# Cross-attention of a decoder trunk: additions ahead of the maximum, probabilities scaled on ScalarE, value mix in four column groups, query units in turn

## What is computed

```python
def mem_xattn(h, mk, mv, wq, wo):
    q = (h @ wq).reshape(b, L, XA_HEADS, XA_HEAD_DIM)
    s = einsum('blhd,bmhd->bhlm', q, mk) * XA_HEAD_DIM ** -0.5
    p = softmax(s, axis=-1)
    o = einsum('bhlm,bmhd->blhd', p, mv).reshape(b, L, D_MODEL)
    return o @ wo

x = x + mixer(rmsnorm(x)); x = x + mem_xattn(rmsnorm(x), ...)
```

## Time and profile before

| | us |
|---|---|
| median of 3 runs | 2808.32 |
| the runs | 2815.7, 2808.32, 2801.9 |
| the profiled execution | 2788.76 |
| its span, first to last instruction | 2786.6 |
| mean granted TensorE clock in it | 0.952 of 2.4 GHz |

### The profile page before, as it was taken

One profiled execution on the slowest core, in us unless ns is written; L12 is line 12 of the kernel. 1 busy time (PEld: TensorE's weight loads), 2 busy tenths in 40 slices (PEclk: granted clock), 3 DMA queues, 4 the chain that ended last, 5 costly groups with the idle time before them and its releaser, 6 DMA issues.

```text
span 2786.6 us, 38288 instructions
## 1 busy us (share of the span) xinstructions
PE 2486.7 (89%) x15517; PEld 2338.8 (84%) x15517; DVE 1469.3 (53%) x2201; ACT 586.2 (21%) x1123; POOL 847.7 (30%) x415
## 2 busy tenths in 40 slices
PE   5989999999999887887998899989989986988787
PEld 5989999999999877776887898889779876867775
DVE  4464553332333546546665745656575666545654
ACT  3431110000000321113223303221330233221113
POOL 0034443334433322221223333333323232412220
PEclk7999999999999999998999999999999997999998
DMA  4641111111111132221101121211112011232221
GB/s 143 203 129 50 42 49 46 46 45 45 45 45 50 36 130 90 77 98 51 49 21 54 51 60 31 65 32 46 46 57 55 22 46 49 99 101 80 80 78 74
DMA packets 242704, 182.20 MB, mean 65 GB/s; under 512 B 6125, under 2 KB 229629, under 8 KB 241503
## 3 DMA queue, kind: packets, MB, share of 16 engines
q1 hardware_dynamic: 197592, 124.87, 15.1%
q10 hardware_dynamic: 44975, 55.41, 5.8%
HBM read 159.97 MB, written 20.98 MB: 65 GB/s over the span
## 4 chain that ended last, share of the span: by engine, by line
PE 75%; DVE 15%; ACT 4%; issue 3%; POOL 1%; DMA 1%; ACTq 0%; SPq 0%; DVEq 0%; POOLq 0%
PE acc L792 33%; PE acc L817 12%; PE acc L991 6%; PE acc L1019 4%; PE acc L917 2%; PE M L1146 2%; PE acc L1225 2%; PE acc L1236 2%; DVE cache L2132 2%; PE acc L1088 2%; PE M L1067 1%; PE acc L1241 1%; DVE x L2056 1%; PE acc L841 1%; PE acc L1229 1%
## 5 line engine op out<-in xcount | busy, mean ns | idle before, releaser
L649 POOL TENSOR_TENSOR w_hi<-w_raw,zero 128x1024 fp32r<-128x1024 f32 x153 | 298.2, 1949 | 1645.9 <-PE acc L792 669.0
L792 PE MATMUL acc<-h_hi,w_hi 128*128 128x344 f32 x2232 | 506.1, 336 | 31.7 <-POOL w_lo L652 21.0
L792 PE MATMUL acc<-h_lo,w_hi 128*128 128x344 f32 x2232 | 481.4, 325 | 0.0
L792 PE MATMUL acc<-h_hi,w_lo 128*128 128x344 f32 x2232 | 476.9, 322 | 0.0
L792 PEld LDWEIGHTS acc<-h_hi,w_hi 128*128 128x128 f32 x2232 | 383.7, 192 | 57.3 <-issue 34.0
L652 POOL TENSOR_TENSOR w_lo<-w_raw,w_hi 128x1024 fp32r<-128x1024 f32 x153 | 395.0, 2582 | 12.0
L792 PEld LDWEIGHTS acc<-h_lo,w_hi 128*128 128x128 f32 x2232 | 385.5, 193 | 0.0
L792 PEld LDWEIGHTS acc<-h_hi,w_lo 128*128 128x128 f32 x2232 | 378.2, 191 | 0.0
L1871 DVE TENSOR_TENSOR x<-acc,x 128x1032 f32<-128x1032 f32 x96 | 117.9, 1231 | 242.0 <-PE acc L817 242.0
L991 PE MATMUL acc<-y_hi,w_hi 128*128 128x344 f32 x384 | 129.8, 338 | 61.5 <-DVE x L2056 57.7
L991 PEld LDWEIGHTS acc<-y_hi,w_hi 128*128 128x128 f32 x384 | 73.2, 191 | 73.5 <-DVE x L2056 59.5
(11 more groups left out here) (307 smaller groups left out, 4673.9 us busy)
## 6 DMA issues: line engine op xcount, KB each, us to landing
w_raw<-in_w_in_even SPq DMA_DIRECT2D x48, 512.0 KB, 3.6
w_raw<-in_w_in_odd SPq DMA_DIRECT2D x41, 512.0 KB, 3.7
cache<-in_cache_mem_k ACTq DMA_DIRECT2D x8, 2048.0 KB, 7.4
cache<-in_cache_mem_v ACTq DMA_DIRECT2D x8, 2048.0 KB, 7.7
w_raw<-in_w_xa_k SPq DMA_DIRECT2D x16, 512.0 KB, 4.3
w_raw<-in_w_xa_v SPq DMA_DIRECT2D x16, 512.0 KB, 3.9
w_raw<-in_w_out_even SPq DMA_DIRECT2D x16, 512.0 KB, 3.7
w_raw<-in_w_xa_q SPq DMA_DIRECT2D x16, 512.0 KB, 3.9
```

Of the source, the lines that this page charges most:

```text
L649: pool.tensor_tensor(hi, raw_ap, zcol.to_broadcast([P, width]), ALU.add).then_inc(w_hi_done, 1)
L792: ins = pe.matmul(acc[a][:, n * 512:n * 512 + CH], wt[:, s, w], mv[:, k, n * CH:(n + 1) * CH], start=(k == 0 and j == 0), stop=(k == KT - ...
```

## The change

Seven edits, all of them in cross-attention:

- VectorE runs `outputs_out` of a slot ahead of the slot's maximum, no longer behind it; the last two jobs of a head (piece 8) are added in slot 6, straight behind the second copy of the mix, and not in slot 7.
- The scaling of the probabilities by 1/sum goes from VectorE (L2114) to ScalarE, behind the exponential of the next tile and ahead of the copy of pt_hi.
- SAMPLE is spread otherwise: the middle heads begin the products in slot 4 with one token and end with two each in slots 8 and 9; the last head takes one in each of slots 3 to 6 and two each in 7 and 8. Its load of the cached values is issued one slot later.
- The mix with the cached values goes to four column groups: sample token b = 2j + r is computed in rows 32j to 32j+31 of the bank, four matmuls with weights of 32 columns stand next to each other in the program, each for another group. `spt` becomes 32 columns wide per token and lies in q_bc's place; VectorE zeroes it once per head (128x512) and not once per layer.
- The copy behind the mix takes 128 rows, and the turning matmuls (L1152) pick 8 of them.
- The two query units run one behind the other, with `token_sums` between them.
- The memset of spt at the start of each layer's attention is gone.

```diff
-SAMPLE = {... "middle": (0, 0, 0, 2, 1, 1, 1, 1, 1, 1), "last": (0, 0, 0, 2, 2, 2, 2, 0, 0, 0)}
+SAMPLE = {... "middle": (0, 0, 0, 0, 1, 1, 1, 1, 2, 2), "last": (0, 0, 0, 1, 1, 1, 1, 2, 2, 0)}
...
-                for b in range(NB):
+                for r in range(2):
                     for m in range(MT):
-                        ins = pe.matmul(M0[0:NB, 0:HD], spt[:, m, b * NB:(b + 1) * NB], cache[:, b * MT + m, :],
-                                        start=(b == 0 and m == 0), stop=(b == NB - 1 and m == MT - 1))
+                        for j in range(NB // 2):
+                            b = 2 * j + r
+                            ins = pe.matmul(M0[32 * j:32 * j + 32, 0:HD], spt[:, m, b, :], cache[:, b * MT + m, :],
+                                            start=(r == 0 and m == 0), stop=(r == 1 and m == MT - 1))
...
-                project_pair((0, 1), attended, KT * (n_th - 1), sums)
+                project(0, attended, KT * (n_th - 1))
+                sums()
+                project(1)
...
+                        if 1 <= i <= TT:
+                            j = i - 1
+                            act.wait_ge(rinv_ready, 8 * n + j + 1)
+                            act.activation(prob[:, j % 2, :], prob[:, j % 2, :], ACT.Copy, scale=rinv[:, j:j + 1]).then_inc(prob_ready, 1)
...
-                        if i == (TT - 1 if kind == "last" else TT + 1):
+                        if i == (TT if kind == "last" else TT + 1):
                             act.wait_ge(ss_ready, n + 1)
                             load_cache(cv_, h, v_loaded)
...
-                    copy(sp[0:NB, :], M0[0:NB, 0:HD], so_ready)
+                    copy(sp[:, :], M0[:, 0:HD], so_ready)
...
                     for i in range(TT + 2):
+                        if i < 7:
+                            outputs_out(i)
                         if i < TT:
                             ... maximum, scaled negative
-                        if i < 7:
-                            outputs_out(i)
-                        if i == 7:
-                            outputs_out(8)
                         if 1 <= i <= TT:
                             ... reciprocal
-                            dve.tensor_scalar(prob[:, j % 2, :], prob[:, j % 2, :], rinv[:, j:j + 1], None, ALU.mult).then_inc(prob_ready, 1)
                         if i == 6:
                             mix_out(0, 0)
                             outputs_out(7)
                             mix_out(0, 1)
+                            outputs_out(8)
...
+                    dve.wait_ge(ss_ready, n + 1)
+                    step(dve.memset(spt[:, :, :, :], 0.0))
```

More of the change, by code:

```diff
@@ L83 @@
          "middle": {8: (0,), 10: (1,), 11: (2,), 13: (3,), 14: (4,), 15: (5,)}, "last": {}}
-SAMPLE = {"first": (0, 0, 0, 0, 1, 1, 1, 1, 2, 2), "middle": (0, 0, 0, 2, 1, 1, 1, 1, 1, 1), "last": (0, 0, 0, 2, 2, 2, 2, 0, 0, 0)}
+SAMPLE = {"first": (0, 0, 0, 0, 1, 1, 1, 1, 2, 2), "middle": (0, 0, 0, 0, 1, 1, 1, 1, 2, 2), "last": (0, 0, 0, 1, 1, 1, 1, 2, 2, 0)}
 def kind_of_head(h):
@@ L233, in build @@
         row_out = Area(a.at)("row_out", [P, D])
+        spt_at = a.at + 4096
         q_bc = a("q_bc", [P, NB, HD])
@@ L240, in build @@
         sp = a("sp", [P, NM])
-        spt = a("spt", [P, MT, NB * NB])
+        spt = Area(spt_at)("spt", [P, MT, NB, 32])
         s4 = a("s4", [P, 4])
@@ L1151, in attention @@
                 for k in range(2):
-                    ins = pe.matmul(M1[:, k * NB:(k + 1) * NB], sp[0:NB, k * P:(k + 1) * P], ident[0:NB, 0:NB],
-                                    start=True, stop=True)
+                    ins = pe.matmul(M1[:, k * NB:(k + 1) * NB].rearrange("p (j r) -> p j r", r=2), sp[:, k * P:(k + 1) * P],
+                                    ident.rearrange("p (j r) -> p j r", r=32)[:, :, 0:2], start=True, stop=True)
                 ins.then_inc(so_turned, 1)
@@ L2112, in attention @@
                             dve.reciprocal(rinv[:, j:j + 1], rsum[:, j:j + 1]).then_inc(rinv_ready, 1)
-                            dve.wait_ge(rinv_ready, 8 * n + j + 1)
-                            dve.tensor_scalar(prob[:, j % 2, :], prob[:, j % 2, :], rinv[:, j:j + 1], None, ALU.mult).then_inc(prob_ready, 1)
                         if i == 6:
@@ L2150, in attention @@
                     after(12)
+                    dve.wait_ge(ss_ready, n + 1)
+                    step(dve.memset(spt[:, :, :, :], 0.0))
                     dve.wait_ge(sp_turned, n + 1)
-                    dve.tensor_copy(spt[:, :, 0:NB * NB:NB + 1], M1[:, 0:MT * NB].rearrange("p (m b) -> p m b", m=MT)).then_inc(spt_ready, 1)
+                    dve.tensor_copy(spt[:, :, :, :].rearrange("p m (j r) c -> p m j (r c)", r=2)[:, :, :, 0:34:33],
+                                        M1[:, 0:MT * NB].rearrange("p (m j r) -> p m j r", m=MT, r=2)).then_inc(spt_ready, 1)
                     after(13)
@@ L2167, in cross @@
                 queries(1, 1)
-                step(dve.memset(spt[:, :, :], 0.0))
                 for h in range(HEADS):
```

## The result

The changed kernel takes 2685.88 us (median of 4 runs, 2684.59 to 2689.7) where the kernel before takes 2811.24 (median of 4, 2801.9 to 2815.7): a ratio of 0.9561, 95% interval 0.954 to 0.9582. The profiled execution has 2687.11 us (span 2685.3), so it stands inside the spread of the runs. That of before, 2788.76, stood outside: its other runs began at 2801.9. Between the two profiled executions lie 101.7 us, between the medians 125.4. The sum of the prediction was 103.6.

A forecast was written before the change was run, and what follows sets the result against it. TensorE holds 75% of the chain, in the heads waiting on VectorE's additions behind the maximum, elsewhere on POOL. Gains 14 + 35.6 + 12 + 2.0 + 40 = 103.6 us off the 2808.3 median: 2705, range 2692 to 2715, overall 2688 to 2745.

The forecast's parts named there:

- The sum of the prediction: Gains in cross-attention added up: 14 + 35.6 + 12 + 2.0 + 40 = 103.6 us.
- more gain than the sum: Waits left standing at turns 6 and 7 go too: 2680 to 2692 us, chance 0.03.
- Part 1: Queries ahead of the heads: units in turn end TensorE's wait for POOL's second split; gain 14 us.
- Part 2: Head slots: additions ahead of the maximum, scaling on ScalarE; 8.9 us per middle head, 6.0 per last head, 47.6 in all.
- Part 3: Wait of 5.20 us at turn 6 and the first heads: sum 2.0 us, bounds -4 and +8.
- the other branch: Turn 6: no product gets ahead of POOL; gain 0.3 us in a middle head, -1.1 in a last one.
- Part 4: Mix with cached values: four column groups overlap, 7.00 us becomes 2.0; gain 5.0 x 8 heads = 40 us.
- rival 1: Mix: matmuls start in program order whatever their group, mix takes 3.5 us, 12 us lost: 2717 us; chance 0.17.
- rival 2: Heads: the VectorE-ScalarE ring binds earlier, slots with products or additions take 4.4 and not 3.7 us: 2726; chance 0.15.
- rival 3: Mix: the column groups don't overlap at all, 40 us less gain: 2745 us; chance 0.07.
- rival 4: Heads: POOL holds ScalarE's scaling as it holds VectorE's products; slower than before, 2829 us; chance 0.03.
- rival 5: Heads: VectorE is in a low half when jobs end, banks come free as late as before: 2752 us; chance 0.03.

The follow-up runs named there:

- old_spread: The changed kernel with the old spread of products (four in slot 3, last head's load of cached values where it was): 2701.27 us, ratio 0.9621.
- scale_on_dve: The changed kernel with the scaling of probabilities back on VectorE, behind the reciprocal and ahead of the low half: 2689.06 us, ratio 0.9559.
- groups_in_a_row: The changed kernel with the mix's loops turned round, all four matmuls of a column group one behind the other: 2706.27 us, ratio 0.9628.
- before_again: The kernel before, unchanged, measured and traced once more: 2811.22 us, ratio 1.0017.
- two_in_slot3: The kernel before with two products in slot 3 of middle and last heads instead of four: 2799.27 us, ratio 0.9977.

## Why the prediction failed

**The step that failed** is the base: "The median of the runs is 2808.3, 0.7% above it with no row that says why, so I take the gain off the median: 2705." The sum was made on an execution without a fall of the clock in slot 4; the traced executions near the median have three to six of them, 9 to 19 us. The change takes the wait behind which they come out of the four middle heads and shortens it to 1.93 us in the last two; its own trace has no fall in slot 4. So its gain against the median is the sum and these falls, and the profiled execution's own time less the sum, 2788.8 - 103.6 = 2685, is close to what the changed kernel runs at. The few us that the longer executions of before have elsewhere aren't taken away: all else took 3.4 us more in the changed kernel's trace too. The prediction had that number and set it aside. It also gave "more gain than the sum" 0.03.

A row of before would have warned me. It has such a fall behind its longer wait, the 5.20 us of the earlier trace rows. The chain of waits of before, 14 matmuls behind that wait and the next 14:

```profile
1177.86 3.20 PE acc L1019 x14
...
1181.28 2.21 PE acc L1019 x14
```

The window 1177 to 1182 has a granted clock of 0.70, that from 1182 on 1.00. So a wait there cost its length and 1 us behind it, and I priced all waits at their length. What was missing in the base is that price behind the 3.26 us wait, 3.0 to 3.4 us a head, paid in three of the four traced executions and not in the one that I read. It isn't a fixed price: in the changed kernel and in old_spread a fall ahead of a further wait left the head no longer.

**Part 1** held: 13.7 us for 14, first scores 27.4 and 27.3 us behind the first matmul. VectorE's last low half was in time.

**Part 2** held in its size: slots 0 to 5 of a middle head gave 9.0 us (forecast 9.5), and slot 6 gave back 0.8 (forecast 0.6; TensorE's row ahead of the mix shows 0.54 of it as a wait). That is 8.2 for 8.9. The last heads wait 1.93 us in slot 4 behind the product that POOL holds, and slot 4 is 2.2 us longer than in a middle head; I had charged 2.9 with what follows. The scaling row was mis-sized, 0.50 us and not 0.38:

```profile
L1579 ACT ACTIVATE prob<-M,nmx,rstd 128x256 f32<-128x256 f32 x64 | 36.2, 565 | 169.1 <-DVE nmx L2114 160.0 <-PE acc L1079 9.1
L1598 ACT ACTIVATE prob<-prob,rinv 128x256 f32<-128x256 f32 x64 | 31.9, 499 | 26.7 <-DVE rinv L2119 26.7
L1331 ACT ACTIVATE pt_hi<-acc 128x256 fp32r<-128x256 f32 x64 | 23.8, 371 | 0.6 <-PE acc L1079 0.5
```

It cost little, because the next instruction starts 0.40 behind it. The estimate of 0.49 from the Trainium skill (ScalarE: Activation LUTs, "What ACT_TABLE_LOAD costs") was the better one. Its rule in "Rules for kernel authors", that a multiplication belongs on VectorE, agrees with one pair of runs: with the products out of POOL's way VectorE's place is 9 us faster, of which the heads explain 6. At the changed kernel the two places can't be told apart (2689.1 and 2685.9).

**Part 3** stood on which product meets POOL, and went the way I had left open: one product gets ahead, one is held. For that branch I had 2.0 us in a middle head. From the start of slot 7's scores to the head's end 46.5 us became 39.35, of which 5.1 are the mix's, so turns 6 and 7 gave 2.0; the forecast of 1.1 was the middle of the two branches. In the last heads they gave nothing (+0.1 and -0.2 us, where that branch had 1.4). So the 103.6 stood nearer to the trace than its terms: part 2 was too large by 0.7 a middle head and part 3 too small by 0.9, which is luck. scale_on_dve shows the other branch, with 3.87 us of wait.

**Part 4** held: 5.1 us in a middle head for 5.0, starts in fours. In the first heads the mix took 2.73 and 3.31 us, with a granted clock of 0.70 and 0.58, behind waits of 1.53 and 3.17 us for the sample rows' scaling, and TensorE waits 0.51 us there for the wider copy (0.46 for the narrow one before). Program order among column groups (rival 1) doesn't hold in groups_in_a_row; the Trainium skill (TensorE: Matmul & The Clock Gate, "The mechanism") has matmuls start strictly in order, and the count of 20 steps in place of 26 speaks against it, as 1021.69 in the earlier trace rows does.

**The rivals**: slots 1 to 5 of a middle head are 2.9 to 3.8 us long and not 4.4 (rival 2), starts in fours leave no room for rival 3, no scaling on ScalarE is held by POOL (rival 4: 64 of them take 492 to 509 ns), and the banks come free in time (rival 5). The first heads gained 5.4 and 2.9 us for a forecast of 3.7 each.

## What to carry to other kernels

A wait can cost more than its length: look at the durations and the granted clock of the matmuls behind it, at whether the same wait has the same price in every repetition, and at whether a further wait behind it takes up what the slower matmuls cost. When the profiled execution is shorter than the runs, first ask what the runs may have that it lacks; if the change removes the cause, take the gain off the profiled execution's own time. An instruction that can be held by another engine is best moved to where that engine is idle, before one asks which engine should run it.

## What the runs showed of the hardware

- TensorE's clock, behind waits of the same length to the hundredth (3.26 us in the kernel before, 2.62 in old_spread), was granted in full in some heads and fell in others, in one execution (0.50 over the 18 matmuls in before_again, 0.65 over them in two heads of old_spread). In the executions of before the three heads of a layer always went alike; in two_in_slot3 and old_spread they didn't.
- Matmuls of two column groups run side by side where the program has them two places apart, by the count of 12 pairs in 20 steps in groups_in_a_row. With the groups interleaved four run side by side: 1.86 us for the 32 passes, for 7.00 in one group.
- An ACTIVATE with a scale from memory took 499 ns where a copy of the same shape from PSUM took 371, but the next instruction on ScalarE started 0.40 us behind its start.
